# First block of a two-block network on one Trainium2 core: projections, window attention, gates and matrix memory as one stream of steps placed by planned durations

## The reference, cut to what matters

```python
p = rmsnorm(x, norm_mix_g) @ w_in            # 2824 columns, cut into the parts below
# 8 query heads, 2 key heads, window 128, one learned sink per head:
s = q @ k.T * 64**-0.5 - slope * dist        # -1e30 outside the window
m = max(max(s), sink);  pr = exp(s - m) / (sum(exp(s - m)) + exp(sink - m));  o = pr @ v
# matrix memory (4 heads of 128): q, k through a causal convolution of width 4 and silu
gates = cumulative sums, running maxima and exponentials of 8 columns of p
h = chunkwise recurrence over C += decay * k.T @ v, times sigmoid(mo)
x = x + concat(o, h) @ w_out
x = x + cross_attention(...); x = x + conv_ffn(...)
mod = silu(c_2) @ w_ada_2 + b_ada_2          # 3072 numbers, first used in block two
```

## Time and profile before

| | us |
|---|---|
| median of 3 runs (2787.48 to 2796.32) | 2794.58 |
| the profiled execution, its own time | 2795.58 |
| its span, first to last instruction | 2793.7 |
| mean granted TensorE clock, share of full | 0.939 |
| PE busy | 2533.4 (91%) |
| DVE busy | 1438.5 (51%) |
| ACT busy | 937.4 (34%) |

### The profile page before, as it was taken

The page is one execution under the profiler, slowest core; times in us unless marked ns, Lnnn a source line. Parts: engine busy times, 40 slices in busy tenths (PEclk is TensorE's granted clock), DMA queues, the critical chain, the costliest instruction groups (busy, mean ns, idle before and its releaser), DMA issues.

```text
span 2793.7 us, 40671 instructions
## 1 busy us (share of the span) xinstructions
PE 2533.4 (91%) x17602; PEld 2046.9 (73%) x17602; DVE 1438.5 (51%) x2444; ACT 937.4 (34%) x1572; POOL 82.2 (3%) x61
## 2 busy tenths in 40 slices
PE   4997878898988999999999998988999999589879
PEld 3785656787777878888888886756777777377757
DVE  5725665537332465544555545745344454666653
ACT  3323342224332333332333324354222232233341
POOL 0000000000000000000000000002000000200000
PEclk9998986889999999999999999978999999699989
DMA  4331110444411233333333333322312320211033
GB/s 133 90 100 47 55 35 16 128 144 118 131 46 53 68 92 97 98 95 98 96 97 98 97 96 109 113 73 76 110 58 62 99 62 24 102 38 38 10 117 117
DMA packets 370810, 233.00 MB, mean 83 GB/s; under 512 B 9796, under 2 KB 344772, under 8 KB 370504
## 3 DMA queue, kind: packets, MB, share of 16 engines
q1 hardware_dynamic: 367896, 224.83, 27.0%
q10 hardware_dynamic: 2736, 5.57, 0.5%
HBM read 211.50 MB, written 18.87 MB: 82 GB/s over the span
## 4 chain that ended last, share of the span: by engine, by line
PE 76%; DVE 14%; ACT 7%; issue 2%; DMA 1%; SPq 0%; DVEq 0%; ACTq 0%
PE PS L1171 17%; PE PS L1172 17%; PE PS L1173 17%; PE PS L1506 4%; PE PS L1157 3%; PE PS L1191 1%; DVE SR L1636 1%; PE PS L1193 1%; PE PS L1192 1%; ACT SR L2239 1%; PE PS L1211 1%; DVE SB L1676 1%; PE PS L1354 1%; PE PS L1424 1%; DVE SB L1760 1%
## 5 line engine op out<-in xcount | busy, mean ns | idle before, releaser
L1171 PE MATMUL PS<-SR 128*128 128x512 f32 (+2 forms) x2384 | 960.7, 403 | 50.2 <-DVE SR L1636 34.0
L1172 PE MATMUL PS<-SR 128*128 128x512 f32 (+2 forms) x2384 | 937.5, 393 | 0.0
L1173 PE MATMUL PS<-SR 128*128 128x512 f32 (+2 forms) x2384 | 935.9, 393 | 0.0
L1636 DVE TENSOR_TENSOR SR<-SB,SR 128x1024 fp32r<-128x1024 f32 (+2 forms) x328 | 395.3, 1209 | 455.6 <-ACT SR L2239 455.4
L1171 PEld LDWEIGHTS PS<-SR 128*128 128x128 f32 (+1 forms) x2384 | 457.1, 192 | 176.9 <-issue 39.0
L1173 PEld LDWEIGHTS PS<-SR 128*128 128x128 f32 (+1 forms) x2384 | 456.3, 191 | 97.2
L1172 PEld LDWEIGHTS PS<-SR 128*128 128x128 f32 (+1 forms) x2384 | 457.5, 192 | 90.9 <-issue 2.2
L2239 ACT ACTIVATE SR<-SB 128x1024 fp32r<-128x1024 f32 (+2 forms) x328 | 337.6, 1035 | 306.0 <-DMA SB<-in_w_down 110.2
L1157 PE MATMUL PS<-SB 128*128 128x128 f32 (+3 forms) x680 | 114.1, 308 | 73.1 <-DVE SB L1804 41.3
L1506 PEld LDWEIGHTS PS<-SB 64*64 64x64 f32 x4096 | 127.5, 135 | 37.6 <-issue 21.9
L1157 PEld LDWEIGHTS PS<-SB 128*128 128x128 f32 (+3 forms) x680 | 85.6, 157 | 92.9 <-DVE SB L1804 45.1
(11 more groups left out here) (237 smaller groups left out, 2599.1 us busy)
## 6 DMA issues: line engine op xcount, KB each, us to landing
SB<-in_w_in SPq DMA_DIRECT2D x110, 512.0 KB, 4.0
SB<-in_w_up SPq DMA_DIRECT2D x88, 512.0 KB, 3.9
SB<-in_w_out SPq DMA_DIRECT2D x32, 512.0 KB, 3.8
SB<-in_w_down SPq DMA_DIRECT2D x32, 512.0 KB, 3.6
SB<-in_w_ada SPq DMA_DIRECT2D x24, 512.0 KB, 4.8
asides<-SB SPq DMA_DIRECT2D x40, 256.0 KB, 4.5
SB<-in_wkv SPq DMA_DIRECT2D x16, 512.0 KB, 3.9
SB<-in_wq SPq DMA_DIRECT2D x16, 512.0 KB, 3.7
```

Source lines behind the costliest of these rows:

```text
L1171: pe.matmul(out, whi[:, k - k0, :], hi[k], start=(k == 0), stop=False)
L1172: pe.matmul(out, whi[:, k - k0, :], lo[k], start=False, stop=False)
L1173: i = pe.matmul(out, wlo[:, k - k0, :], hi[k], start=False, stop=(k == j.K - 1))
L1636: v.tensor_tensor(m.f32r(a, kn * cn), m.f32(a, kn * cn), m.f32r(a + 1024, kn * cn).bitcast(F32), SUB).then_inc(*on("split.v", p))
```

## The change: what it does

1. **One call of `flow`** takes everything from the first projection to the end of `mlstm`. The main stream is `proj_a(0)`, `proj_m(0)`, `proj_a(1)`, `proj_m(1)`, then all 24 `ada_mm`. Side streams are the gates, the norm `mix1`, three lanes that share the list of 16 attention units, and two of `mlstm` (heads 0, 2 and 1, 3). Attention may start once the first half's projections are done (`opened`), not after `proj_a(1)`. `out0`, `out1`, `kx` and what follows have no `ada_mm` among them any more.
2. **Steps are cut finer**: `win_s` into `win_s`, `win_x`, `win_p`; `ml_e` into `ml_e`, `ml_x`; `ml_c` into `ml_c`, `ml_h`; the tanh and the product of `ev_conv_m` become `conv_t` and `conv_o`, placed between the matmuls of the next tile.
3. **Bias and maximum fused**: one `tensor_tensor_reduce` for each head writes the negated sum and its minimum. The scale 0.125 moves into the read-out of `aq`, the exponential takes the scale -1. The four products with the reciprocal become one over 1024 columns. A third buffer for the probabilities.

```diff
+        self.Pv, self.PTv = ([work(a, 1024) for a in x] for x in ((2048, 3072, 6144), (4096, 5120)))
...
+        job(f"aq{h}", w, 0, 128, 4, src, ok, "copy", "gemm.a", scale=0.125, dst=lambda t, h=h: m.aqT[:, t, hs(h)])
...
+            "win_s": [("pe", 0.9), ("v", 2.0)], "win_x": [("a", 3.0)], "win_p": [("v", 1.6)],
...
+        "ada_mm": [("pe", 1.8)], "ev_gate": [("v", 0.7)], "ev_conv_m": [("a", 0.6), ("v", 2.9)],
...
-        self.together(chain(proj_a(0), proj_m(0)), self.rms("mix1"))
-        self.mark("ha")
-        self.run(proj_a(1))
-        self.emit(("alibi",))
...
-        attn = staggered([self.window(n, jp) for n in range(8) for jp in range(2)], 3)
-        self.run(partly(proj_m(1), attn, 0.3))
-        self.mark("g")
-        self.together(self.gates(), attn)
-        self.mark("att")
-        ada = self.ada()
-        self.run(partly(staggered([self.mlstm(h) for h in range(4)], 2), ada, 0.1))
+        units = [(n, jp) for n in range(8) for jp in range(2)]
+        self.flow(chain(proj_a(0), proj_m(0), self.opened(), proj_a(1), self.flagged("a1"), proj_m(1),
+                        self.flagged("g", ("mark", "g")), self.ada()),
+                  self.gates(), self.rms("mix1", self.room), *[self.windows(units) for _ in range(3)], self.attended(),
+                  self.mlstm(0, 2), self.mlstm(1, 3))
...
-        self.run(partly(T("out0"), ada, 0.5))
+        self.run(T("out0"))
...
-        self.together(partly(T("out1"), ada, 0.25), chain(self.rms("mem"), self.rms("x0")))
+        self.together(T("out1"), chain(self.rms("mem"), self.rms("x0")))
...
-        self.run(ada)
...
-        v.scalar_tensor_tensor(out=P, in0=s, scalar=0.125, in1=bias, op0=MUL, op1=ADD).then_inc(*on("win.v", "bias", *key))
-        w.wait_ge(*at("win.v", "bias", *key))
-        v.tensor_reduce(mx, P, AX.X, MAX).then_inc(*on("win.v", "max", *key))
+        for g in range(4):
+            i = v.tensor_tensor_reduce(out=P[:, g, :], in0=s[:, g, :], in1=bias[:, g, :], scale=-1.0, scalar=3e38, op0=ADD,
+                                       op1=MIN, accum_out=mx[:, g:g + 1])
...
-        for g in range(4):
-            i = v.tensor_scalar(P[:, g, :], P[:, g, :], sm[:, g:g + 1], None, MUL)
-        i.then_inc(*on("win.v", "p", *key))
+        v.tensor_tensor(P, P, sm.unsqueeze(2).to_broadcast([128, 4, 256 if n else 128]), MUL).then_inc(*on("win.v", "p", *key))
```

More of the change, by code:

```diff
@@ L597, in flow @@
             for step in steps:
+                if step[0] == "slab" and not self.slabs[step[1]][5]:
+                    self.steps.append(step)
+                    continue
                 chained = step[0][:3] == "ev_" or step[0] == "hs_sum"
@@ L707, in rms @@
         yield [("rms_sum", tag, b, free)]
+        yield from room((self.pairs, 1))
         b, free = self.pairs.take()
@@ L715, in rms @@
         self.pairs.give(b, ("rms.v", "o", tag, 7))
+        self.done.add(tag)
         return steps
@@ L730, in window @@
     def window(self, n, jp):
+        u = 2 * n + jp
+        yield from self.after("ha", *[("ws", u - 1)] * (u > 0), *["a1"] * (n > 3))
+        yield from self.room((self.pairs, 1), (self.P, 1))
+        self.done.add(("ws", u))
         b, free = self.pairs.take()
@@ L733, in window @@
         st = self.stat()
-        self.pairs.give(b, ("win.v", "bias", n, jp))
+        self.pairs.give(b, ("win.v", "max", n, jp))
         yield [("win_s", n, jp, b, free, p, pfree, st)]
+        yield [("win_x", n, jp, p, st)]
+        yield [("win_p", n, jp, p, st)]
+        if u:
+            yield from self.after(("wt", u - 1))
+        yield from self.room((self.pairs, 1), (self.PT, 1))
+        self.done.add(("wt", u))
         b, free = self.pairs.take()
@@ L743, in window, with windows, attended @@
         self.banks.give(b, ("win.a", "o", n, jp))
-        return [("win_o", n, jp, b, free, q)]
+        yield [("win_o", n, jp, b, free, q)]
+        self.done.add(("win", u))
+    def windows(self, units):
+        while units:
+            yield from self.window(*units.pop(0))
+    def attended(self):
+        yield from self.after(*[("win", u) for u in range(16)])
+        self.done.add("att")
+        yield [("mark", "att")]
     def gates(self):
+        yield from self.after("g")
+        yield from self.room((self.pairs, 1))
         b, free = self.pairs.take()
@@ L753, in gates @@
         yield [("gates_exp",)]
+        yield from self.room((self.banks, 1))
         b, free = self.banks.take()
         self.banks.give(b, ("gates.v", "mc"))
[L756 to L778, removed]
+        yield [("gates_t", b, free)]
@@ new lines, in gates, with mlstm @@
+        self.done.add("gates")
+    def mlstm(self, *heads):
+        for h in heads:
+            yield from self.after("att", "gates")
+            for first, second, e, f in (("ml_e", "ml_q", ("ml.v", "e", h), ("ml.v", "dec", h)),
+                                        ("ml_s", "ml_k", ("ml.v", "sc", h), ("ml.a", "kt", h))):
+                for name, event in ((first, e), (second, f)):
+                    yield from self.room((self.pairs, 1))
+                    b, free = self.pairs.take()
+                    self.pairs.give(b, event)
+                    yield [(name, h, b, free)]
+                    if name == "ml_e":
+                        yield [("ml_x", h)]
+            for c in range(8):
+                yield from self.room((self.banks, 1 + (c < 7)))
+                b, free = self.banks.take()
+                b2, free2 = self.banks.take() if c < 7 else (None, None)
+                if c < 7:
+                    self.banks.give(b2, ("ml.v", "C", h, c))
+                yield [("ml_c", h, c, b, free, b2, free2)]
+                self.banks.give(b, ("ml.v", "h", h, c))
+                yield [("ml_h", h, c, b)]
+            yield from self.room((self.pairs, 1))
+            b, free = self.pairs.take()
+            self.pairs.give(b, ("ml.v", "mix", h))
+            yield [("ml_o", h, b, free)]
@@ L780, in cross, with opened, flagged @@
+    def opened(self):
+        ha = ("upto", "pe", "ha")
+        for i in range(3):
+            self.P.give(i, ha)
+        for i in range(2):
+            self.PT.give(i, ha)
+        self.done.add("ha")
+        yield [("mark", "ha"), ("alibi",)]
+        yield from self.after("mix1")
+    def flagged(self, name, *steps):
+        self.done.add(name)
+        yield list(steps)
     def cross(self, n):
@@ L1781, in win_s @@
         P, s = v3(m.Pv[p], 4)[:, :, 0:W], v3(pair(b), 4)[:, :, 0:W]
-        bias, sinks = v3(m.alib[:, 1024 * jp:1024 * jp + 1024], 4)[:, :, 256 - W:256], m.row("sinks", 4 * jp, 4 * jp + 4)
+        bias = v3(m.alib[:, 1024 * jp:1024 * jp + 1024], 4)[:, :, 256 - W:256]
         mx, nm, sm, es = stats(st, 4)
+        if not n + jp:
+            w.wait_ge(*at("rows", 0))
+            v.tensor_scalar(small[:, 496:504], m.row("sinks"), -1.0, None, MUL).then_inc(*on("win.v", "sinks"))
         w.wait_ge(*at("win.pe", "s", *key))
```

75 lines of the change are left out of this document (46 added, 29 removed), and 1 row of the table wide.

## The result

The changed kernel takes **2768.22 us** (median of 4, 2765.73 to 2776.36), the kernel before 2793.76 beside it: a ratio of 0.9917, interval [0.9891, 0.9943]. The profiled execution took 2765.73, 29.85 less than the profiled one of before. The forecast was 2767, in the range 2710 to 2797. The time is right, but in part by luck: two terms of the sum are off by 13 and 16 us, in opposite directions, and cancel.

What follows compares the result with a forecast made beforehand. The prediction followed PE as the bounding engine and summed -22.5 + 66.3 - 9.5 - 60.5 - 2.0 = -28.2 us from 2795.6 to 2767.4, 2766.4 as a median, stated as 2767; range 2710 to 2797.

Steps and rivals of the forecast that it cites:

- End of `mo1`: First matmul to the end of `mo1`: 305 us of PE work plus 21 lost; net -22.5 us after the later start.
- the nearest row is a stretch of block two that the same planner placed: Up to `mo1`: block two's 8.5% loss to idle and half clock, taken as 15 us on the 176 beside attention.
- 4, because DVE is short there: Beside attention: 4 us of loss added, since DVE has 66 us of work against PE's 62.
- End of `mo1` to `ml_q`: From `mo1` to `ml_q`: 24 `ada_mm` at half clock and other steps sum to 105.8 us, +66.3.
- hidden under the first 20 `ada_mm`: Behind `mo1`: the gates' own chain, some 36 us before, runs beneath the `ada_mm` block.
- `mlstm`: Up to `out0`: wait and two `ada_mm` pairs gone, other changes called even; -9.5 us (0 to -15).
- `out0` to `q0`: Stretch without its 20 `ada_mm`: 151.1 us, -60.5; first `kx` tiles may wait 0 to 8 us.
- The rest: From `q0` on: same steps, same order, no term; only -2.0 us for the first tile of `q0`.
- A: Rival in the stretch behind `mo1`: `ada_mm` mostly at full clock, giving 2713 us; chance 0.13.
- B: Rival beside attention: idle time moves instead of going, a loss of 45 to 53 gives 2791 to 2799; chance 0.08.
- C: Rival beside attention: early transposes and late DVE reads hold PE, 72 us lost, giving 2818; chance 0.09.
- D: Rival in attention: the fused pass does not pay; its 11 us of DVE got no term, no chance given.

Runs made afterwards that it cites:

- e11_old_order: The kernel before, in its own order, plus the fused pass and single `ada_mm` behind tiles of `out0`, `out1`, `kx`, none in `mlstm`: 2745.5 us, ratio 0.9840.
- e1_later: The changed kernel with no `ada_mm` in the planned stream; 12 stand in `out0`, 8 in `out1`, 4 ahead of `q0`: 2750.6 us, ratio 0.9866.
- e12_early: The changed kernel with its block of 24 `ada_mm`, but `ada_c` behind `av1` instead of the last unit's exponentials: 2759.3 us, ratio 0.9897.
- e6_unfused: The changed kernel, order kept, with bias and minimum as two wide passes and four products with the reciprocal: 2765.6 us, ratio 0.9900.
- e8_fused: The kernel before with only the fused pass, the scale in the read-out of `aq` and the one wide product: 2775.4 us, ratio 0.9929.

## Why the prediction was right, step by step

**"End of `mo1`": the size of the loss was wrong.** The forecast was 305 us of work and 21 of loss; the stretch took 312.2. In it PE was busy 310.2 us at a clock of 1.00 and idle 2.0:

```profile
43.66:355.90 312.24, 310.21 (x1690) 247.60 (x1690) 182.67 (x391) 124.83 (x282) 0.00 (x0) 1.00 0.28 77
```

So the work was counted about 5 us short, and the loss was 2, not 21 and less than the lower bound of 8. The step that failed is "the nearest row is a stretch of block two that the same planner placed", which gave 15 of the 21: its idle time and its clock of 0.95 did not carry over to this stretch. The "4, because DVE is short there" was not there either. The fused pass was taken at 0.47 us and has 0.42 and 0.08 for its accumulator.

**"End of `mo1` to `ml_q`": right, 106.7 for 105.8**, with its parts: the wait 4.3 (4.4), `ada_mm` 82.2 in all (80), two `ml_e` 7.2 (7.1), `gates_f` 3.6 (3.5). But the sentence that the gates' chain is "hidden under the first 20 `ada_mm`" hid a loss: without the block the stretch is 30 us, so the block bought almost nothing by covering it: 82.2 of `ada_mm` and 4.3 of wait cost 76.6.

**"`mlstm`", -9.5: right in the number**, 79.7 us, but the sum's "I call that even" is not shown. In e11_old_order, the old order without `ada_mm` in `mlstm`, it takes 76.5, that is 12.7 less than before. The planned order is 3.2 longer than that, although both `ml_e` of the first heads are already done. By these two profiles, an overestimate and an underestimate of about 3 us cancel here as well.

**"`out0` to `q0`", -60.5: wrong by 15.6.** The step that failed took "0 to 8" for the tiles of `kx` at 0 and one wait of 1.3 for the sum of `x0`. That wait was 6.7, the stretch from `kx` to `q0` is 66.3 where I had 59, and `out1` 54.0 where I had 46.5. I named the cover that the 20 `ada_mm` give to the norm's chain and to the splits, and gave it no price. e1_later, with 20 of them back among the tiles, has 12.3 us of these waits instead of 20.5. But the lost cover is not all of it. The kernel before, with its 20 there, already had 17.3 us of these waits (4.1 for norm sums, 13.2 for splits), and `kx` with `vx0` and `vx1` is at a clock of 0.92 as before, where I had taken 2 us off for it. So the sum also set waits and a clock that were there before at too little.

**"The rest", -2.0, was -6.7**: the same steps, with PEclk 0.98 instead of 0.95 in the first 268 us behind `q0`, in which PE gets 22 matmuls further. I had only 2 of it, for the first tile of `q0`. Over the fourteen profiled executions this part, always the same steps, takes 2054 to 2067 us.

**The rivals.** A, `ada_mm` at full clock, is refuted: 0.52 in the block, and 0.53 in e12_early where PE has no gap at all. The rule of the Trainium skill behind it ("TensorE: Matmul & The Clock Gate", section "Why this matters for your kernels": gaps between bursts drop the clock) describes a cause, but not the only one: a gap of 4.3 us does stand ahead of the fall in the changed kernel, and none ahead of the fall in e12_early. Here the measurement decides. B and C did not come: the transposes' 30.6 us of waits are gone, not moved; PE's waits from 205 to 356 add up to 0.8 us. D, that the fused pass has no term, is true in the new order (e6_unfused) and would have been false in the old one (e8_fused, -14 us beside attention).

So the change is three things with signs of their own, by the ratios: the fused pass alone 0.9929, with the planned stream and `ada_mm` in pairs at about the old places 0.9866, with the block 0.9917. The first two give 1.3% together, and the block takes 0.5% back. How the 1.3% divide depends on the order in which they are added, since the fused pass is worth nothing that can be told in the planned stream.

## What to carry to other kernels

Give filler work a place by what it would cover: here the 24 `ada_mm` went from 3.2 us each in a block (76.6 in all) to 1.2 each, one behind every tile of a stretch in which PE waits for norms and splits. A term "hidden" in a sum needs the price of the stretch without its cover, or the sum holds a loss that nobody sees. And the worth of a faster pass is measured in the order in which it will run: 14 us in one, at most 2 in the other.

## What the runs showed that I had not expected

Two `ada_mm` in a row among dense tiles cost clock, one hardly does: PEclk 0.87 against 0.95 over the same 1063 matmuls, 12 us in 200. The granted clock stays at half from 362 to 454 in e12_early, while PE is busy without a gap, some nine tenths of it with matmuls of one column or with four partitions. And in the profile of that run, 4.3 us less idle time ahead of the block brought `ml_q` 8.5 us forward, since the first pair and `gates_f` then ran nearly all at full clock.
